# A second half for the weight ring, a lower threshold for VectorE's rests, and bias tile copies moved into the gate loop

## The reference

```
# first block, layer 0: conv + attention mixer, then peer; layer 1: sparse attention mixer, then peer
x = x + g1 * mixer(modulate(rms_norm(x), sh1, sc1))
x = x + g2 * peer_ffn(modulate(rms_norm(x), sh2, sc2), w_q, keys, u, v)
# peer_ffn, per token: 8 heads, top 16 of 128 keys in each half, top 16 of the 256 sums
eid = ...                       # 8 x 16 experts out of 16384
a = gelu(x . u[eid]);  out = sum(softmax(scores) * a * v[eid])
# second block, twice
x = x + 0.5 * g1 * rmsnorm(swiglu(h1, w_gate, w_up, w_down))      # D_FF = 2816
x = x +       g2 * rmsnorm(hybrid_mixer(h2, ...))                 # attention with relative bias
x = x + 0.5 * g3 * rmsnorm(swiglu(h3, w_gate, w_up, w_down))
# shifts, scales and gates: silu(c) @ ada_w + ada_b
```

## Time and profile before

| what | us |
|---|---|
| median of 3 runs | 3270.36 (3262.22 to 3277.01) |
| the profiled execution's own time | 3260.61 |
| its span, first to last instruction | 3258.6 |
| PE busy in it | 3132.0 (96%) |
| DVE, ACT, POOL busy | 2305.7, 1620.5, 683.2 |
| mean granted clock of PE | 0.99 |

### The profile page before, as it was taken

The page is one execution under the profiler, slowest core; times in us unless marked ns, Lnnn a source line. Parts: engine busy times, 40 slices in busy tenths (PEclk is TensorE's granted clock), DMA queues, the critical chain, the costliest instruction groups (busy, mean ns, idle before and its releaser), DMA issues.

```text
span 3258.6 us, 61534 instructions
## 1 busy us (share of the span) xinstructions
PE 3132.0 (96%) x21286; PEld 2839.7 (87%) x21286; DVE 2305.7 (71%) x4210; ACT 1620.5 (50%) x3026; POOL 683.2 (21%) x678
## 2 busy tenths in 40 slices
PE   6999999999999999999999999999998999999998
PEld 5779999988887866899998888889988999998998
DVE  6549878877777345897887777777666767766754
ACT  1224468864444354455886444444454434445443
POOL 0108835520000100484553000000010010000000
PEclk9999999999999999999999999999999999999999
DMA  7635554468887322454445787767543785754354
GB/s 282 241 126 174 192 195 135 135 209 264 262 265 231 126 95 78 145 185 154 137 135 193 244 263 264 259 222 268 203 165 118 263 275 202 265 194 134 131 183 146
DMA packets 176618, 632.09 MB, mean 194 GB/s; under 512 B 23624, under 2 KB 23632, under 8 KB 175728
## 3 DMA queue, kind: packets, MB, share of 16 engines
q1 hardware_dynamic: 134416, 491.48, 44.2%
q0 software_dynamic: 42064, 139.07, 13.2%
q10 hardware_dynamic: 16, 0.01, 0.0%
HBM read 627.21 MB, written 9.50 MB: 195 GB/s over the span
## 4 chain that ended last, share of the span: by engine, by line
PE 77%; DVE 12%; DMA 5%; DVEq 2%; ACT 2%; issue 1%; SPq 0%; ACTq 0%
PE ps L648 21%; PE ps L489 10%; PE ps L491 9%; PE ps L490 9%; PE ps L477 6%; DMA ring<-stream 4%; PE ps L627 2%; PE ps L629 2%; PE ps L628 2%; PE ps L524 2%; PE ps L1041 2%; PE ps L1040 2%; DVE unit_low L1570 1%; DVE r_outT L2128 1%; DVE r_outT L2122 1%
## 5 line engine op out<-in xcount | busy, mean ns | idle before, releaser
L1570 DVE TENSOR_TENSOR unit_low<-ring,unit_high 128x1024 fp32r<-128x1024 f32 x560 | 738.8, 1319 | 251.9 <-ACT unit_high L1128 244.0
L1128 ACT CAST unit_high<-ring 128x1024 fp32r<-128x1024 f32 x604 | 632.1, 1046 | 372.7 <-DMA ring<-stream 260.8
L491 PE MATMUL ps<-expert_x_high,unit_low 128*128 128x256 f32 x1968 | 552.3, 281 | 0.0
L489 PE MATMUL ps<-expert_x_high,unit_high 128*128 128x256 f32 x1552 | 449.7, 290 | 15.7 <-DVE unit_low L1570 15.2
L490 PE MATMUL ps<-expert_x_low,unit_high 128*128 128x256 f32 x1552 | 437.2, 282 | 0.0
L491 PE MATMUL ps<-norm_parts,unit_low 128*128 128x256 f32 x1504 | 424.2, 282 | 0.0
L491 PEld LDWEIGHTS ps<-expert_x_high,unit_low 128*128 128x128 f32 x1968 | 372.4, 189 | 0.0
L648 PE MATMUL ps<-unit_low,expert_high 128*128 128x512 f32 x1024 | 324.2, 397 | 2.5 <-DVE unit_low L1570 2.5
L648 PE MATMUL ps<-unit_high,expert_low 128*128 128x512 f32 x1024 | 321.9, 395 | 0.1
L648 PE MATMUL ps<-unit_high,expert_high 128*128 128x512 f32 x1024 | 318.0, 392 | 0.9 <-ACT unit_high L1128 0.8
L489 PEld LDWEIGHTS ps<-expert_x_high,unit_high 128*128 128x128 f32 x1552 | 296.0, 191 | 21.4 <-DVE unit_low L1570 14.1
(11 more groups left out here) (330 smaller groups left out, 7271.8 us busy)
## 6 DMA issues: line engine op xcount, KB each, us to landing
ring<-stream SPq DMA_DIRECT2D x914, 512.0 KB, 3.5
score<-ada POOLq DMA_DIRECT2D x128, 512.0 KB, 5.1
arena<-ada POOLq DMA_DIRECT2D x96, 512.0 KB, 4.8
arena<-bias_tiles POOLq DMA_DIRECT2D x48, 192.0 KB, 2.7
arena<-ada SPq DMA_DIRECT2D x8, 1024.0 KB, 17.3
bias_tiles<-bias_rows POOLq DMA_DIRECT2D x8, 768.0 KB, 19.1
x_home<-x POOLq DMA_DIRECT2D x2, 1024.0 KB, 6.1
x<-x_home POOLq DMA_DIRECT2D x2, 1024.0 KB, 8.8
```

The costliest lines, as they stand in the source:

```text
L489: pe.matmul(out, hi[:, kt, :], xh[:, kt, :], start=(kt == 0), stop=False)
L491: mm = pe.matmul(out, lo[:, kt, :], xh[:, kt, :], start=False, stop=(kt == KD - 1))
L1128: nc.scalar.copy(hi, ring[:, unit % SLOTS, :]).then_inc(whi_ready, 1)
L1570: V.tensor_tensor(out=lo, in0=ring[:, unit % SLOTS, :], in1=hi, op=ALU.subtract).then_inc(wlo_ready, 1)
```

## The change

It does three things.

- **Ring.** From ffn0's first unit on (`first_late` = 598) the ring has eight slots. Four new ones lie in `arena` (`ring_late`), the other four are the old ones. SP may load unit u once unit u-8 is used; the first four late units are issued with no wait of their own, directly behind unit 597. The cuts of `arena` are put in another order so that the four slots lie where the second block keeps nothing. The loops of PE and ACT in the feed-forward phases handle eight units per pass in place of four, since the slot repeats every eight.
- **Steps.** `PLAIN_STEPS` is 72; the number of rests made in `step` is capped so that it still ends with unit 57.
- **Bias copies.** POOL issues the eight copies one at a time, behind the one-hots of g = 5, 11, ..., 47 of peer0's gate loop.

```diff
-PLAIN_STEPS = 77
+LATE_SLOTS = 2 * SLOTS
+PLAIN_STEPS = 72
...
+        ring_late = flat[:, late_at:late_at + SLOTS * UNIT].rearrange("p (s n) -> p s n", s=SLOTS)
+        wlo_late = over("unit_low_late", "arena", [P, SLOTS, UNIT], late_at)
...
+        loaded_late = [sem(f"unit_loaded_late{s}") for s in range(LATE_SLOTS)]
...
+        first_late = start.get("ffn0", units)
+
+        def slot_in(here, late_here, unit):
+
+            k = (unit - first_late) % LATE_SLOTS
+            if unit < first_late or k >= SLOTS:
+                return here[:, (unit if unit < first_late else first_late + k) % SLOTS, :]
+            return late_here[:, k, :]
...
-            rounds = units // SLOTS
+            rounds = first_late // SLOTS
             with sp.Fori(1, rounds) as i:
                 for s in range(SLOTS):
                     sp.wait_ge(unit_done, i * SLOTS + (s - SLOTS + 1))
                     sp.dma_start(ring[:, s], stream[i * SLOTS + s]).then_inc(loaded[s], 16)
...
+            rounds = (units - first_late) // LATE_SLOTS
+            for k in range(min(LATE_SLOTS, units - first_late)):
+                if k >= SLOTS:
+                    sp.wait_ge(unit_done, first_late + k - LATE_SLOTS + 1)
+                sp.dma_start(raw_of(first_late + k), stream[first_late + k]).then_inc(loaded_late[k], 16)
+            if rounds > 1:
+                with sp.Fori(1, rounds) as i:
+                    for k in range(LATE_SLOTS):
+                        sp.wait_ge(unit_done, i * LATE_SLOTS + (first_late + k - LATE_SLOTS + 1))
+                        sp.dma_start(raw_of(first_late + k), stream[i * LATE_SLOTS + (first_late + k)]).then_inc(loaded_late[k], 16)
...
# PE, ffn
-                with pe.Fori(1, NF // 2) as i:
-                    for e in range(2):
-                        column(e, i)
+                with pe.Fori(0, NF // 4) as i:
+                    for c in range(2, 6):
+                        column(c, i)
...
-                with pe.Fori(0, 4) as i:
-                    for e in range(4):
-                        pe.wait_ge(hlo_ready, i * 4 + (NF * no + e + 3))
-                        spread(u + 2 + e, n + 2 + e, i, 4, i * 4 + (2 + e), False, False)
+                with pe.Fori(0, 2) as i:
+                    for e in range(8):
+                        pe.wait_ge(hlo_ready, i * 8 + (NF * no + e + 3))
+                        spread(u + 2 + e, n + 2 + e, i, 8, i * 8 + (2 + e), False, False)
...
# DVE, peer, step
-                    if steps[0] >= PLAIN_STEPS:
+                    if steps[0] >= PLAIN_STEPS and lows[0] < DIRECT + 2:
                         low(u + lows[0], n + lows[0])
                         lows[0] += 1
...
# POOL, peer
                 G.memset(arena[:, DIRECT:NE - 8, :], 1.0).then_inc(ones_ready, 1)
-                if l == 0:
-                    for c in range(8):
-                        rows4 = bias_rows[4 * c:4 * c + 4]
-                        src = bass.AP(rows4.tensor, rows4.offset + P - 1, [[512, 4], [-1, P], [1, TW]])
-                        pool.dma_start(bias_tiles[4 * c:4 * c + 4], src).then_inc(bias_shifted, 16)
                 wait_used(pool, start[ph] + PH + DIRECT - 1)
...
                     m.then_inc(hot_ready, 1)
+                    if l == 0 and g % 6 == 5 and g < 48:
+                        rows4 = bias_rows[4 * (g // 6):4 * (g // 6) + 4]
+                        src = bass.AP(rows4.tensor, rows4.offset + P - 1, [[512, 4], [-1, P], [1, TW]])
+                        pool.dma_start(bias_tiles[4 * (g // 6):4 * (g // 6) + 4], src).then_inc(bias_shifted, 16)
```

More of the change, by code:

```diff
@@ L198, in program @@
         nb = cut(4 * TW).rearrange("p (e a b) -> p e a b", e=2, a=2)
+        conv_t = cut(2 * S).rearrange("p (a b) -> p a b", a=2)
+        og_at = used[0]
+        cumrow = cut(8 * S).rearrange("p (a b) -> p a b", a=8)
+        gates = cut(TT * 48).rearrange("p (a b) -> p a b", a=TT)
+        gsum = cut(TT * 48).rearrange("p (a b) -> p a b", a=TT)
+        blk = cut(2 * CMP_LEN * 2 * NCMP).rearrange("p (a l c n) -> p a l c n", a=2, l=CMP_LEN, c=2)
+        late_at = used[0]
+        assert og_at % 8 == 0 and late_at % 8 == 0 and late_at >= og_at + 2 * KD * S and late_at >= sum_at + 2 * NF * S
+        kcv = cut(4 * S).rearrange("p (a b) -> p a b", a=4)
+        qs_all = cut(8 * S).rearrange("p (a b) -> p a b", a=8)
+        ftmp = cut(4 * S).rearrange("p (a b) -> p a b", a=4)
+        assert used[0] == late_at + SLOTS * UNIT
+        cum = cut(S)
         hsq = cut(S)
@@ L426, in parts_of @@
             four = n >= split0["ffn0"] or any(0 <= n - split0[ph] < DIRECT - NPLAIN for ph in ("peer0", "peer1"))
-            return (extra if four and n % 4 >= 2 else whi)[:, n % 2, :], wlo[:, unit % SLOTS, :]
+            return (extra if four and n % 4 >= 2 else whi)[:, n % 2, :], low_of(unit)
         def wait_used(eng, unit, it=0, per=0):
@@ L459, in _ @@
                     sp.dma_start(ring[:, s], stream[i * SLOTS + s]).then_inc(loaded[s], 16)
-            for u in range(rounds * SLOTS, units):
+            for u in range(rounds * SLOTS, first_late):
                 sp.wait_ge(unit_done, u - SLOTS + 1)
                 sp.dma_start(ring[:, u % SLOTS], stream[u]).then_inc(loaded[u % SLOTS], 16)
+            rounds = (units - first_late) // LATE_SLOTS
[8 more added lines that the diff above has]
+                        sp.dma_start(raw_of(first_late + k), stream[i * LATE_SLOTS + (first_late + k)]).then_inc(loaded_late[k], 16)
+            for u in range(first_late + rounds * LATE_SLOTS, units):
+                sp.wait_ge(unit_done, u - LATE_SLOTS + 1)
+                sp.dma_start(raw_of(u), stream[u]).then_inc(loaded_late[(u - first_late) % LATE_SLOTS], 16)
             sp.wait_ge(x_ready, KD * len(phases))
@@ L1127, in high @@
                 wait_unit(act, unit, it, per)
-                nc.scalar.copy(hi, ring[:, unit % SLOTS, :]).then_inc(whi_ready, 1)
+                nc.scalar.copy(hi, raw_of(unit)).then_inc(whi_ready, 1)
             def have(func):
@@ L1569, in low @@
                 dve.wait_ge(whi_ready, it * per + (n + 1))
-                V.tensor_tensor(out=lo, in0=ring[:, unit % SLOTS, :], in1=hi, op=ALU.subtract).then_inc(wlo_ready, 1)
+                V.tensor_tensor(out=lo, in0=raw_of(unit), in1=hi, op=ALU.subtract).then_inc(wlo_ready, 1)
             def norm_low(ph, xl, xh, freed=None):
@@ L2283, in low @@
                 pool.wait_ge(whi_ready, n + 1)
-                G.tensor_tensor(out=lo, in0=ring[:, unit % SLOTS, :], in1=hi, op=ALU.subtract).then_inc(wlo_ready, 1)
+                G.tensor_tensor(out=lo, in0=raw_of(unit), in1=hi, op=ALU.subtract).then_inc(wlo_ready, 1)
             def bias(e, f, head):
```

68 lines of the change are left out of this document (35 added, 33 removed).

## The result

The kernel after takes 3228.9 us in the median of four runs (3227.1 to 3233.3), the kernel before 3269.1 in the same comparison; the ratio is 0.9865 with the interval [0.9837, 0.9893]. Six more runs of the kernel after gave a median of 3232.0 (3227.0 to 3235.2) at a ratio of 0.987 [0.984, 0.9901]. All ten together have a median of 3229.7. The gain is 40 us in the medians of the first comparison; the interval of its ratio leaves room for 35 to 53 us, and in the comparison with the six runs, where before had 3276.6, the medians are 45 us apart. The forecast was 3235.4 with a gain of 35.0.

A forecast was written before the change was run, and what follows sets the result against it. PE was busy 96% of the span, so only its stalls, including waits for DVE's rests, could be won. 9.4 - 1 + 8.1 - 1 + 15.5 + 4.0 = 35.0 us off the 3270.4 median gave 3235.4; range 3218 to 3252.

The forecast's parts named there:

- Step 72: Routing end of peer0 and peer1: earlier rests remove the unit 48 stall; 4.7 us each, 9.4 us, less 1 for dips.
- One dip in three: New waits ahead of unit 58, two in all: one in three halves the clock, costing 1 us; bounds 0 and 3.4.
- Bias copies out: Last units before peer0's gate loop: without the copies the stretch equals peer1's, gaining 8.1 us; lower bound 5.
- Bias copies in the gate loop: peer0's gate loop: POOL's idle time and ACT's lead mostly cover single copies; cost 1 us, bounds 0 and 17.
- Eight slots: Loads seven units ahead cover late landings: ffn0 to ffn2 gain 15.5 us (8 to 17), hyb0 4.0 (0 to 4.5).
- Loops of eight: Feed-forward loops of PE and ACT: same instructions in half the turns, 0 us.
- Bandwidth (1): Feed-forward phases lack bandwidth, not slots; part of the 19.5 us stays, say 13: 3248 us. Chance 0.07.
- Refetched loops (2): Feed-forward phases: PE's 384-instruction loop is fetched anew each turn, 36 to 66 us over 20 turns: 3271 to 3301. Chance 0.05.
- The sign named for it, one or two packets: Expected in the changed profile: one or two instruction packets over the feed-forward loops; more, with idle at turns, would mean refetching.
- Copies as dear in the new place (3): peer0's gate loop: late loads shut ACT in beside bias copies, costing 17 us: 3252 us. Chance 0.05.
- A worse end of the routing (4): Both peers: routing ends 1.5 us later each, or both new waits dip the clock: 3241 us. Chance in full 0.05.
- No effect (5): Change doesn't do what it says, as casts still wait for PE unit by unit; ring's 19.5 us gone: 3255. Chance 0.02.

The follow-up runs named there:

- the guarded version: Kernel after with VectorE's ten rests spread over steps 72 to 85 and POOL's fill of ones issued only after VectorE's last integer fetch: 3223.9 us, ratio 0.9851.
- version four units ahead: Kernel after, eight slots and loops of eight kept, but each load waits for the unit four ahead instead of eight: 3254.7 us.
- version five ahead: Kernel after, eight slots kept, but each load waits for the unit five ahead instead of eight: 3229.4 us, one execution.
- the steps alone: Kernel before with only VectorE's ten rests moved to start from step 72: 3260.6 us against 3270.4, ratio 0.9949.
- the crowded run: Kernel after with its eight bias copies issued behind eight consecutive groups of one-hots instead of every sixth: 3260.0 us, one execution.
- the run with the fill in pieces: Kernel after with VectorE's ten rests spread over steps 72 to 85 and POOL's fill of ones cut into eight: 3223.0 us, ratio 0.9849.

## Why the prediction was right

The mechanism held, and the size nearly: 35.0 forecast, 40 measured in the medians, and each part where it was put.

- *Step 72*: forecast 9.4 - 1. PE has no wait at unit 48 and no half clock behind it. A wait of 1.46 + 0.68 = 2.1 us in peer1 and 1.9 in peer0 stands ahead of unit 58, forecast as 2.1 to 2.8, and neither halved the clock. One dip in three was somewhat too dear: of the sixteen such waits in the eight profiles with rests from step 72 on and not spaced, three had half clock behind them. From the end of unit 47 to the start of unit 58 peer1 gained 4.5 us, forecast 4.7. The part alone was worth 9.8.
- *Bias copies out*: 8.1, measured 8.6 alone. Together with step 72, units 48 to 63 of peer0 went from 62.7 to 49.5 us, 13.2 against 4.7 + 8.1 = 12.8. Rows of peer1 were the right measure for peer0.
- *Bias copies in the gate loop*: 1, measured 0. The cover of two units, 7.4 us, was reckoned too small: it counts to ACT's cast, and PE needs the unit one unit later. That leaves 3 x 3.72 = 11.2 us, and even the slowest crowded load makes it with 8.5 + 1.05 + 1.2 = 10.8 (an estimate from these rows). Of the bounds, the upper one was never near, since what costs is a queue of copies on POOL, and spaced ones don't queue.
- *Eight slots*: 15.5 in the feed-forward phases, measured 4.9 + 5.7 + 4.4 = 15.0. hyb0 4.0, measured 2.2 in the pair of profiles, and 2.0 to 5.1 over all (139.1 to 139.4 us with five or eight units of lead, 141.4 to 144.2 with four). hyb1 is no standard for hyb0 to the last 2 us: hyb0 had half clock near its end in every profile, hyb1 in twelve of fourteen but not in before. Without it hyb1 took 137.4 us in before and 137.6 in the guarded version, with it 138.2 to 139.4. The forecast had taken a lucky row for its standard.
- *Loops of eight*: 0. The version four units ahead shows no gain by them, and leaves room for a loss of 1 to 2 us in ffn1 and ffn2.

**Where it was off.** The gain was set against the median of before, and that was right: the two profiles differ by 27 us only. The number that failed is the one in between, the 3225.6 that the sum gave against the profiled execution's 3260.6; the profile of after has 3233.3. The terms of the sum add up in the trace, and mix1, which has none, is 8.9 us off. It stands above for after; this is its fastest execution, in the version with loads four units ahead (PEclk is the third figure from the right):

```profile
1040.50:1268.60 228.10, 221.56 (x1210) 167.78 (x1211) 106.83 (x412) 97.17 (x310) 18.90 (x52) 0.97 0.29 95
```

Its code is the same in all fourteen profiles, and so is PE's idle time in it, 6.0 to 6.6 us. It takes 228.1 to 238.6 us, by how long the clock stays halved behind its waits: 13.7 us in the fastest, 17.1 in before, 41.0 in after. Eight of the fourteen lie at 231.4 to 232.9. The profile of after had 238.6, that of before 229.7, which accounts for some 8.9 us of the 13 between the traces and the medians, if mix1 is alike in the medians. The rest I leave open; executions of before spread from 3260 to 3296 us, and what makes the slow ones slow no profile of them shows.

**The rivals.** Bandwidth (1) is out by the version five ahead. Refetched loops (2): the queue of instructions carried 5 packets over ffn0's product part, 4 before, with 0.95 us of idle PE in it, where 5 turns at 1.75 us would be 8.8. The sign named for it, one or two packets, was wrong for both kernels. The Trainium skill, "Runtime: NRT & Kernel Launch", section "Instruction fetch mechanics", lets a taken branch outside two pages of 256 instructions wait for a fetch; no such wait is to be seen here. A turn of the loop is 192 matmuls, 192 weight loads and 14 others, so it may have lain within two pages, and that rule is not put to the test. The packets of after:

```profile
q8 instruction: 5, 0.08, 0.2%
```

Copies as dear in the new place (3): out, and crowding them shows what they would cost. A worse end of the routing (4): not here. It did come in peer0 of the steps alone, beside late loads, and a meeting with the fill is a way to a late routing that the forecast didn't have, 17 us dear. No effect (5): out.

## What to carry to other kernels

A ring is judged by its latest load, not its median one: count the units between a load's issue and its use, and add slots until the late ones fit; here one more slot did what four did. When work is moved out of an engine's tail, look at what then stands bare behind it, and mix the moved instructions with those that have nothing to wait for. A long instruction of POOL should start only when VectorE has passed the operations that it can hold; here a wait on a semaphore that existed already did that at no measurable cost.

## What the runs showed of the hardware that was not expected

VectorE was held by GpSimd for whole instructions: conversions and integer operations with a tensor in SBUF lasted 2.3 to 2.6 us beside one of POOL's rests of 2.4, and 12, 16.2 and twice 13.8 us beside its fill of 13.8, where they take 0.2 to 1.3 us by themselves. The Trainium skill, "SBUF — State Buffer", section "Who interferes with whom", says that a VectorE copy, cast or `tensor_scalar` in a two-port mode and a GpSimd instruction exclude each other, the second one waiting for the whole of the first, while a two-input `tensor_tensor` contends only with GpSimd's reads. The trace agrees in both: while the fill, which reads nothing, ran from 1459.52 to 1473.33 in the kernel after, VectorE's two-input operations took their 0.69 and 1.23 us as elsewhere, and one of them took 2.49 us instead of 0.28 beside a rest, which reads two tiles.

What happens where two instructions of POOL follow each other without a gap stays open. In the crowded run the conversion begun at 375.62 beside the last rest (375.61 to 378.01) was not let in between that rest and the fill behind it, but held through both, 16.22 us. In the run with the fill in pieces it began 0.18 us behind the start of the last rest, and it ended 0.15 us behind that rest's end, with the first piece already following (DVE, then POOL):

```profile
374.17 2.35 DVE L2159 CAST pick<-r_ab 128x256 f32<-128x256 uint32 x1
...
373.99 2.39 POOL L2329 TENSOR_TENSOR unit_low<-ring,unit_high_early 128x1024 fp32r<-128x1024 f32 x1 [0.19 <-ACT unit_high_early L1167]
376.32 7.22 POOL L2405 MEMSET arena<- 128x2048 f32 x4
```

So a hold can run on into the next instruction, and need not. What decides it is not shown.

A bias copy of 768 KB issued from POOL's queue takes 14.4 to 15.1 us with no other copy beside it, and the eighth of a close row of them held POOL for 13.27 us in issuing (31.09 in the kernel before). In the gate loop that was nearly the whole cost of the crowded copies, 12.4 us of waiting PE out of 13.2; the slower loads beside them cost next to nothing.
